# Two tiles' expert picking moved from in front of the second block's mix to behind it

## What is computed

```
h = rms_norm(x, n_mix_pre) * (1.0 + sc1) + sh1
m = mixer(h)      # short convolution and gated linear attention, merged, projected
x = x + g1 * rms_norm(m, n_mix_post)
h = rms_norm(x, n_ffn_pre) * (1.0 + sc2) + sh2
x = x + g2 * rms_norm(peer(h), n_ffn_post)
```

```
s = einsum('thpd,hpkd->thpk', q, subkeys)          # q = (xb @ wq) in 8 heads x 2 halves
sv, si = top_k(s, 16)
cand = sv[:, :, 0, :, None] + sv[:, :, 1, None, :]
cand_id = si[:, :, 0, :, None] * 128 + si[:, :, 1, None, :]
top_v, top_i = top_k(cand, 16)
expert = take_along_axis(cand_id, top_i); gate = softmax(top_v)
act = gelu(einsum('thkd,td->thk', u_tab[expert], xb))
out = einsum('thk,thkd->td', gate * act, v_tab[expert])
```

## Time and profile before

| | us |
|---|---|
| three runs | 4278.25 (median), 4275.8 to 4285.69 |
| the profiled execution | 4286.02, span 4284.2 |
| PE busy | 3212.9 (75%) |
| DVE busy | 2494.9 (58%) |
| POOL busy | 1650.3 (39%) |
| ACT busy | 802.7 (19%) |
| transfers of the gather's queue | 1140.92 MB, 66% of 16 engines' span |
| mean granted TensorE clock | 0.799 |

### The profile page before, as it was taken

The page is one execution under the profiler, slowest core; times in us unless marked ns, Lnnn a source line. Parts: engine busy times, 40 slices in busy tenths (PEclk is TensorE's granted clock), DMA queues, the critical chain, the costliest instruction groups (busy, mean ns, idle before and its releaser), DMA issues. The chain is left out here.

```text
span 4284.2 us, 46731 instructions
## 1 busy us (share of the span) xinstructions
PE 3212.9 (75%) x15781; PEld 1741.5 (41%) x15781; DVE 2494.9 (58%) x7734; ACT 802.7 (19%) x1299; POOL 1650.3 (39%) x1380
## 2 busy tenths in 40 slices
PE   5999996975688777776788776777666666766676
PEld 2888896865265542531255342243111111111111
DVE  3345554238854646778764655677785555555554
ACT  4232333342123122110123112110000100000000
POOL 2211103634355543543355544353333333333332
PEclk7999998977799887977899897788666666676666
DMA  8111003434899999999999999999999999999998
GB/s 331 44 62 60 33 24 117 143 110 147 333 372 381 386 379 372 371 367 369 371 399 410 389 394 381 379 399 363 383 391 405 410 413 406 407 415 409 409 412 341
DMA packets 225110, 1358.92 MB, mean 317 GB/s; under 512 B 28422, under 2 KB 37542, under 8 KB 82668
## 3 DMA queue, kind: packets, MB, share of 16 engines
q0 software_dynamic: 156672, 1140.92, 66.0%
q1 hardware_dynamic: 68204, 215.00, 13.8%
HBM read 1322.48 MB, written 33.35 MB: 316 GB/s over the span
## 5 line engine op out<-in xcount | busy, mean ns | idle before, releaser
L1115 DVE CUSTOM_DVE_ANT_0 peer_uv<-peer_uv,all_PS 128x512 f32<-128x512 f32 x2176 | 1437.6, 685 | 1125.0 <-PE all_PS L1053 584.2
L1053 PE MATMUL all_PS<-peer_hT,peer_sel 96*128 96x512 bf16 x2176 | 984.4, 468 | 850.8 <-DVE peer_halves L1115 787.8
L1036 POOL DMA_INDIRECT peer_uv<-in_uv,peer_idx x1088 | 1045.1, 961 | 1488.6 <-PE all_PS L1073 1176.5
L1053 PEld LDWEIGHTS all_PS<-peer_hT,peer_sel 96*128 96x128 bf16 x2176 | 206.3, 101 | 1670.4 <-DVE peer_halves L1115 1287.0
L1073 PE MATMUL all_PS<-peer_uv,peer_zw 128*32 128x512 f32 x4352 | 829.3, 864 | 2.1 <-DVE peer_zw L1135 2.1
L920 POOL TENSOR_TENSOR flow_w_lo<-flow_w,flow_w_hi 128x1024 fp32r<-128x1024 f32 (+1 forms) x204 | 461.3, 2265 | 531.7 <-ACT flow_w_hi L913 527.0
L1089 ACT ACTIVATE peer_ge<-peer_pre 128x4 f32<-128x4 f32 x272 | 55.9, 205 | 2095.7 <-DVE peer_pre L1121 1934.6
L1073 PEld LDWEIGHTS all_PS<-peer_uv,peer_zw 128*32 128x32 f32 x4352 | 154.4, 142 | 428.8 <-issue 426.4
L940 PE MATMUL all_PS<-mix_h_hi,flow_w_hi 128*128 128x384 f32 (+1 forms) x672 | 282.1, 420 | 35.6 <-POOL flow_w_lo L920 31.7
L913 ACT ACTIVATE flow_w_hi<-flow_w 128x1024 fp32r<-128x1024 f32 (+1 forms) x204 | 203.6, 1004 | 336.6 <-PE all_PS L942 148.3
L941 PE MATMUL all_PS<-early_h_h_low,flow_w_hi 128*128 128x384 f32 (+1 forms) x672 | 225.4, 335 | 0.0
(11 more groups left out here) (294 smaller groups left out, 4693.8 us busy)
## 6 DMA issues: line engine op xcount, KB each, us to landing
cond_w<-in_w_ada SPq DMA_DIRECT2D x12, 2048.0 KB, 11.0
flow_w<-in_w_gate_ab SPq DMA_DIRECT2D x48, 512.0 KB
flow_w<-in_w_query SPq DMA_DIRECT2D x48, 512.0 KB
flow_w<-in_w_conv SPq DMA_DIRECT2D x36, 512.0 KB
peer_uv<-in_uv,peer_idx POOLq DMA_INDIRECT x1088
gla_w<-in_w_heads SPq DMA_DIRECT2D x24, 512.0 KB, 3.8
flow_w<-in_w_proj_b SPq DMA_DIRECT2D x24, 512.0 KB
flow_w<-in_w_out SPq DMA_DIRECT2D x24, 512.0 KB
```

Of the source, the lines that this page charges most:

```text
L1036: self.nc.gpsimd.indirect_dma_start(out=self.uv[:, n % self.NUV, :], out_offset=None, in_=self.A["uv"], in_offset=bass.IndirectOffsetOnAxi ...
L1053: nc.tensor.matmul(PS[:, f, :], self.sel[:, c:c + 1].broadcast_to([3 * GR, P]), self.hT[:, g % self.NH, f * 512:(f + 1) * 512], start=True ...
L1115: nc.vector.tensor_tensor_reduce(part, part, PS[:, f, :], 1.0, 0.0, ALU.mult, ALU.add, self.halves[:, d, f, e:e + 1]).then_inc(M["dotted"], 1)
```

## The change

Pick 0 takes tile 0 alone and has no token between its marks (`marks = [0] * 7`). Through `begin`, GpSimd nevertheless issues the four gathers ahead, and SyncE loads token 0's h rows, as soon as the phase has it in its order. Tiles 1 and 2 (the samples) are picked in a second call of `pick_phase`, which is written behind block 1's mix and in front of its merge, with a share of its own: 88 of 502. The lists of these two tiles live until then in a buffer `rest` at the other end of memory, and `best` and `place` become lists of one view per tile. For block 2 that share is 0, and its marks are as before.

Marks after, by the same formula: pick 0 ends at token 0; block 1's mix at 59, the new pick at 116, merge 147, out 172, norm 198, keys 256, pick 1 320. Block 1's mix is thus 59 tokens (67 before), merge 31 (35), out 25 (28), norm 26 (30), keys 58 (64), pick 64 (72).

```diff
-    def fetch(self, pool, upto):
+    def fetch(self, pool, upto, begin=False):
-        for n in self.steps("pool", upto + self.AHEAD if upto else 0):
+        for n in self.steps("pool", upto + self.AHEAD if upto or begin else 0):
...
-                        last = nc.vector.max(best[0:R[t], t, i, 0:8], s1[0:R[t], i % 2, t, :])
+                        last = nc.vector.max(best[t][0:R[t], i, 0:8], s1[0:R[t], i % 2, t, :])
...
-def pick_phase(nc, A, G, part, gat, best, place, following, brought, lo, hi):
+def pick_phase(nc, A, G, part, gat, chosen, best, place, following, brought, lo, hi):
...
-        PS, nt = G["PS"], len(part.tiles)
-        u0 = part.tiles[0]
+        PS, nt = G["PS"], len(chosen)
+        u0 = part.tiles[chosen[0]]
...
-        early = 0 if part.index else PARTS_OF + 2
-        turns = Turns(lo, hi, NJ - early)
-        upto = lambda j: turns.upto(j - early) if j >= early else lo
+        begin = u0 == 0
+        turns = Turns(lo, hi, NJ)
+        upto = turns.upto
...
+            if begin:
+                gat.turn(sp, 1)
...
-                if j >= early:
-                    gat.fetch(pool, upto(j))
+                gat.fetch(pool, upto(j), begin)
...
-SHARES = (94, 50, 38, 42, 90, 100)
+SHARES = ((94, 88, 50, 38, 42, 90, 100), (94, 0, 50, 38, 42, 90, 100))
...
+                    start = lo
                     if part.index == 0:
-                        marks = [0, 0, 0, 0, 0, 0, 24]
+                        marks = [0] * 7
                     else:
+                        shares = SHARES[part.index - 1]
                         span = gat.before[part.tiles[0]] - lo
-                        marks = [lo + span * sum(SHARES[:i]) // sum(SHARES) for i in range(len(SHARES) + 1)]
+                        marks = [lo + span * sum(shares[:i + 1]) // sum(shares) for i in range(len(shares))]
...
-                                mix_phase(nc, A, G, part, gat, w, w0, h_early, taps, cbias, a_in[0], gates, marks[0], marks[1])
+                                mix_phase(nc, A, G, part, gat, w, w0, h_early, taps, cbias, a_in[0], gates, start, marks[0])
                                 h_early.free()
+                                if part.index == 1:
+                                    pick_phase(nc, A, G, PARTS[0], gat, range(1, len(PARTS[0].tiles)), *waiting, None, None, marks[0], marks[1])
+                                    rest.free()
...
+                            of = [lists[:, :, e] for e in range(nt)]
+                            if part.index == 0:
+                                rest = Early(nc, None, "rest", (("lists", [P, 2, nt - 1, 2 * PH, TOPK], False),))
+                                of[1:] = [rest.tiles[0][0][:, :, e] for e in range(nt - 1)]
+                            best, place = [a[:, 0] for a in of], [a[:, 1].bitcast(U32) for a in of]
...
-                        pick_phase(nc, A, G, part, gat, best, place, following, h_early, marks[5], marks[6])
-                    w0, lo = w0 + len(once), marks[6]
+                        pick_phase(nc, A, G, part, gat, range(nt) if part.index else (0,), best, place, following, h_early,
+                                   marks[-2], marks[-1])
+                        waiting = best, place
+                    w0, lo = w0 + len(once), marks[-1]
```

More of the change, by code:

```diff
@@ L1727, in _ @@
             if part.samples:
-                step(nc.vector.memset(best[:, nt - 1], 0.0))
-                step(nc.vector.memset(place[:, nt - 1], 0))
+                step(nc.vector.memset(best[nt - 1], 0.0))
+                step(nc.vector.memset(place[nt - 1], 0))
             gat.dots(dve, turns.before())
@@ L1736, in _ @@
                     for t in range(nt):
-                        last = nc.vector.max(best[0:R[t], t, i, 0:8], s1[0:R[t], i % 2, t, :])
+                        last = nc.vector.max(best[t][0:R[t], i, 0:8], s1[0:R[t], i % 2, t, :])
                     step(last)
                     for t in range(nt):
-                        nc.vector.max_index(place[0:R[t], t, i, 0:8], best[0:R[t], t, i, 0:8], s1[0:R[t], i % 2, t, :])
-                        last = nc.vector.match_replace(s2[0:R[t], t, :], best[0:R[t], t, i, 0:8], s1[0:R[t], i % 2, t, :], LOWEST)
+                        nc.vector.max_index(place[t][0:R[t], i, 0:8], best[t][0:R[t], i, 0:8], s1[0:R[t], i % 2, t, :])
+                        last = nc.vector.match_replace(s2[0:R[t], t, :], best[t][0:R[t], i, 0:8], s1[0:R[t], i % 2, t, :], LOWEST)
                     step(last)
@@ L1744, in _ @@
                     for t in range(nt):
-                        last = nc.vector.max(best[0:R[t], t, i, 8:16], s2[0:R[t], t, :])
+                        last = nc.vector.max(best[t][0:R[t], i, 8:16], s2[0:R[t], t, :])
                     step(last)
                     for t in range(nt):
-                        last = nc.vector.max_index(place[0:R[t], t, i, 8:16], best[0:R[t], t, i, 8:16], s2[0:R[t], t, :])
+                        last = nc.vector.max_index(place[t][0:R[t], i, 8:16], best[t][0:R[t], i, 8:16], s2[0:R[t], t, :])
                     step(last)
@@ L1760, in lows @@
         return 2 * self.tiles
-def pick_phase(nc, A, G, part, gat, best, place, following, brought, lo, hi):
-    with Phase(nc, f"pick{part.index}", G["flow"]) as sc:
-        PS, nt = G["PS"], len(part.tiles)
-        u0 = part.tiles[0]
+def pick_phase(nc, A, G, part, gat, chosen, best, place, following, brought, lo, hi):
+    with Phase(nc, f"pick{part.index}_{chosen[0]}", G["flow"]) as sc:
+        PS, nt = G["PS"], len(chosen)
+        u0 = part.tiles[chosen[0]]
         sums, sums2 = sc.sb("sums", [P, PH, PAIRED]), sc.sb("sums2", [P, PH, PAIRED])
@@ L1831, in pick @@
             def pick(t, q, step):
-                sv = best[:, t].rearrange("p (h s) k -> p h s k", s=2)
+                sv = best[chosen[t]].rearrange("p (h s) k -> p h s k", s=2)
                 si = places[:].rearrange("p (h s) k -> p h s k", s=2)
                 if q == 0:
-                    step(nc.vector.tensor_copy(places[:], place[:, t]))
+                    step(nc.vector.tensor_copy(places[:], place[chosen[t]]))
                     for at0, a0, a1, width in STRIPS:
@@ L2095, in hybrid_decoder @@
                         lists = mid.sb("lists", [P, 2, nt, 2 * PH, TOPK])
-                        best, place = lists[:, 0], lists[:, 1].bitcast(U32)
                         junk = lists[:].rearrange("p q t s k -> p (q t s k)")[:, 0:D]
```

## The result

| | median | range | runs |
|---|---|---|---|
| before | 4279.41 | 4271.56 to 4618.29 | 20 |
| changed | 4287.76 | 4278.95 to 7754.97 | 20 |

The ratio of the times is 1.0016, with a 95% interval of 1.0008 to 1.0023: 6.9 us slower (3.4 to 9.8); one slow run of each kernel, at 4618.29 and 7754.97 us, is not in the ratio. The forecast was +7 to the median of the first three runs. The other runs of either kernel scatter by some 5 us to each side, at most 9, and the two profiled executions stand only 3.2 us apart in their spans (that of the kernel before was 6.6 us above its median, that of the changed kernel 1.4). So of these 7 us the profiles can place less than half.

What follows compares the result with a forecast made beforehand. The prediction took transfers, gathers of the expert table, to set the pace once the first had landed. Its terms, -80.8 + 159 - 72 + 2 - 1 = +7 us on the median of 4278.25, gave 4285; range 4266 to 4302.

Steps and rivals of the forecast that it cites:

- token 319 done at 2103: Sign at block 1's end: its last token done at 2103 us and not before 2096.
- (a): Tail of pick 0: it goes with its 24 tokens, -80.8 us; their cost moves to block 1's phases.
- the carry-over: Everything behind token 319: marks, order and bytes are unchanged, so its 2172.6 us stay the same.
- (b): New phase behind block 1's mix: two tiles picked beside 57 tokens, 158 us plus 1 for one phase more, +159.
- (c): Block 1's other six phases: 33 tokens fewer, worth 2.18 us each, -72 us.
- (d): Start of block 1's mix: it begins with an empty pipeline and waits for tokens 0 and 1, +2 us.
- (e): End of pick 0: tile 0's expert numbers are written about 1.1 us earlier, -1 us.
- Held issues: Rival, new phase: GpSimd's gather issues grow beside the pick's bf16 work on VectorE, +20 us; chance 0.03.
- limit of 358 GB/s: Rule on a core's HBM share: block 1's phases would already be at the limit, all terms cancel, +0.
- transfers alone: Faster rival: every token costs 2.67 us wherever it stands, -10 us, 4268; chance 0.15.
- dense chain: Slower rival: dense work holds block 1, leaner phases save 1.86 us a token, +20 us, 4298; chance 0.18.
- No effect: Rival: tail and new phase price tokens alike, so all terms cancel, 4278 us; chance 0.09.

Runs made afterwards that it cites:

- e7: The changed kernel with a share of 44 in place of 88 for the new pick phase (31 tokens, not 57): 4281.58 us, ratio to before 1.0001.
- e8: The changed kernel with a share of 140 in place of 88 for the new pick phase (81 tokens, not 57): 4290.63 us, ratio to before 1.0011.
- e4: The kernel before with 48 tokens in place of 24 in the tail of pick 0: 4284.34 us, ratio to before 0.9998.
- e1: The kernel before with tiles 1 and 2 not picked in pick 0's tail, but given copies of tile 0's numbers and gates: 4260.92 us, ratio 0.9939.
- e2: The changed kernel with tiles 1 and 2 not picked in the new phase, but given copies of tile 0's numbers and gates: 4274.52 us, ratio to before 0.9979.
- e3: The kernel before with no token in place of 24 in the tail of pick 0: 4313.4 us, ratio to before 1.0061.
- e9: The changed kernel with other marks in block 1 (mix 65 tokens, new phase 45, pick 1 80): 4283.51 us, ratio to before 0.9997.
- e10: The kernel before, all three tiles picked in front of the mix, with the same tokens per phase as e9: 4280.17 us, ratio to before 0.9990.

## Why the prediction was right, and where its steps were not

**The sum.** The forecast of +7 agrees with the +6.9 of the times, and part of that is luck. The prediction's own sign was token 319 done at 2103; it was done at 2097.5, 1.4 us later than before and not 7. In the windows the sum is -80.8 + 160.7 - 79.3 = +0.6, and the first dot product came 0.8 later. The two profiled executions differ by 3.2 us where the times differ by 7, so more than half of the difference is placed by no trace. What the windows do show is the prediction's mechanism: a large piece removed and a nearly equal one made, because a token costs nearly the same beside a pick and beside dense work.

**(a) and the carry-over.** Right. The tail went, and what stands behind token 319 took 2173.9 us up to the last dot product (2097.5 to 4271.4), where it was 2172.5.

**(b) The new phase.** Forecast 159, measured 160.7; but the value was right by two errors that cancel. Of its 26.1 us a tile and 1.86 a token, e7 and e8 showed 10 and 2.48: 33 us too much for the tiles, 35 too little for the tokens. The slope came from pick 1 and pick 2. But pick 1 at marks 248 to 320 is some 16 us below the line of its own phase in the other kernels, and pick 2 does not lie on that line at all, as the open points above show. Where the pair is carried further it fails: by 10 us in e4's tail, and for the new phase with 31 and 81 tokens it would give 110 and 203 us, measured 96.8 and 220.9. The wait is the one that the prediction named for the tail: buffers come free late. GpSimd's wait in the new phase of the changed kernel (us, times, longest) answers to the earlier trace rows:

```profile
POOL peer_uv L1036 <- PE all_PS L1073: 91.0, 14, 10.8
```

**(c) The six leaner phases.** Forecast -72 at 2.18 a token; with (d) the six took 874.8 for 954.1, so -79.3, and -81 without (d)'s 2: 2.4 to 2.5 a token. e1 and e2, which have the same two dealings, differ by 949.6 - 875.9 = 73.7 us, 2.23 a token. The runs with other counts gave 2.19, 2.32, 2.27 and 2.47, against an assumed 2.18. The size was up to an eighth off; the statement that it is less than a transfer's own price (2.53) held in all of them, in the last by little. Phase by phase the forecast missed by more: merge 117.1 for 105, out 79.9 for 95, norm 80.1 for 86, keys 189.9 for 200, pick 1 207.2 for 197. The first two belong together. The end of the first tile (token 128), with SyncE's loads of h rows and the copy of y, moved from out into merge by the marks, and behind it in SyncE's queue stand the weights. Where token 128 lies in out (the kernel before, e1, e3), out took 29 us more than 2.53 a token; in the seven other kernels in the coarse order it took 16 to 19 more. ScalarE's waits in the merge of the changed kernel:

```profile
ACT flow_w_hi L913 <- DMA flow_w<-in_w_proj_b: 26.1, 4, 10.3
ACT flow_w_hi L913 <- DMA flow_w<-in_w_proj_a: 19.9, 2, 17.9
```

In the merge of the kernel before, the wait for `in_w_proj_b` was 6.4 us. That the queue's order is the cause was read, not tested. The prediction called these moves free; they are, only for the sum of both phases. Pick 1's 10 us too many belong to (b)'s false point: at 2.5 a token, 8 tokens fewer than 72 should have given 20 us less, and as the marks that suited it were gone too, it was 5.

**(d) The start of the mix.** Its mechanism is seen; the timeline of the changed kernel (start, duration, engine, line) stands here:

```profile
1054.28 0.29 DVE L1908 SCALAR_TENSOR_TENSOR peer_idx<-pick_pair 128x128 uint32<-128x128 f32 x1 [1.66 <-ACT peer_gate L1825]
1054.86 1.11 POOL L1036 DMA_INDIRECT peer_uv<-in_uv,peer_idx  x1 [31.68 <-POOLq L143]
1054.93 2.85 ACT L974 ACTIVATE mix_h_hi<-early_h_h 128x1536 fp32r<-128x1536 f32 x2 [0.77 <-PEq L143]
...
1062.01 0.69 DVE L1115 CUSTOM_DVE_ANT_0 peer_uv<-peer_uv,all_PS 128x512 f32<-128x512 f32 x1 [7.44 <-DMA peer_uv<-in_uv,peer_idx]
...
1066.35 3.42 DVE L980 TENSOR_TENSOR early_h_h_low<-early_h_h,mix_h_hi 128x1536 fp32r<-128x1536 f32 x2
1068.21 0.29 PEld L940 LDWEIGHTS all_PS<-mix_h_hi,flow_w_hi 128*128 128x128 f32 x1 [4.74 <-issue]
1068.24 0.66 PE L940 MATMUL all_PS<-mix_h_hi,flow_w_hi 128*128 128x384 f32 x1 [4.26 <-DVE early_h_h_low L980]
```

VectorE waited 7.44 us for token 0 and did the halves of h behind tokens 0 and 1, with TensorE idle for 4.26 us; the first product is 6.2 us behind the first dot product. In the kernel before it stood 6.4 us behind the mark at 1142.0. What the empty pipeline costs thus lies for the most part ahead of the first dot product, and no run measured the +2 by itself. The mix took 200.6 us where 201.3 had been forecast, at a share of 0.94 (0.93 forecast).

**(e) The earlier numbers.** Half right. The numbers were written and the first gather issued 1.1 us earlier against the last step of tile 0's picking, as forecast; by the clock it is 0.6, as the first part was 0.5 us later. But the first dot product came at 1062.01 and not 1061.24: token 0 needed 7.2 us from issue to dot product, against 5.8, and so it was in every kernel of either kind (see e9 and e10). In the changed kernel SyncE issues weights for the mix at 1055.41, in the same moment; that these slow the first gather is likely and was not tested. The term was -1 and came out as +0.2, +0.8 with the first part's delay.

**Held issues and the limit of 358 GB/s.** Neither is seen here. The gather's issue took the same time beside the new pick as anywhere:

```profile
L1036 POOL DMA_INDIRECT peer_uv<-in_uv,peer_idx x58: 932/940/1165, 1261.7 to 1421.8; - x58
```

No trace shows in which of its modes VectorE ran the pick's operations, so this speaks for this pick alone. And e1 and e2 held 419 and 417 GB/s in full windows, with a program on one core; a second core that also transfers was not tried. The rivals "transfers alone" and "dense chain" missed by the price of a token: 2.2 to 2.5, between their 2.67 and 1.86. "No effect" missed by the least, by 7 us; for the place itself e9 and e10 do not exclude it, and with other dealings of the tokens e7 and e9 are level with the kernel before within their intervals.

## What to carry to other kernels

Where a transfer queue is nearly full over the whole stretch, ask of a moved piece of work which unused time of that queue it removes and which it makes; here 74 us became 78. Price a step by pairs of stretches that have more and less of it, but take both from the same phase and measure such a line at three points before carrying it far. And compare places at equal marks: two kernels that differed by 7 us were 3 apart once the same tokens stood in each phase, while dealing VectorE's work more finely gained 15 to 19 us in three of four trials and nothing in the fourth.

## What the runs showed of the hardware

A gathered token of 1.05 MB in 8 KB rows takes 2.53 us (415 GB/s) if nothing is in the way, with the DMA share at 1.01 (e1, e2). The pick's work on VectorE beside it did not lengthen GpSimd's issue (a median of 940 ns with and without). Not expected was how far the start of the gather moves between profiled executions of kernels whose first part is the same: first dot products at 1055.9 to 1067.3 us, which hides changes of a few us in single profiles unless they are read from that point on, or from the first gather's issue where the change touches the time between the two.
